# Moving the reciprocal root of the head norm to GpSimd, in a streaming encoder layer with matrix memory

## The reference, cut to what matters

```python
(C1, n1, m1), hm = mlstm_sequence(carry, (q, k, v, it, lf), n_lead)   # h = num / max(|den|, exp(-m))
mu = jnp.mean(hm, axis=-1, keepdims=True)
hc = hm - mu
hm = hc * lax.rsqrt(jnp.mean(hc * hc, axis=-1, keepdims=True) + EPS)
hm = hm.transpose(0, 2, 1, 3).reshape(B, L, D_M) * g_headnorm * o_gate
branch_m = hm @ w_branch_m
```

## Time and profile before

| what | value |
|---|---|
| time, median of 3 runs | 1316.61 us (1314.5 to 1318.08) |
| the profiled execution | 1317.66 us, span of its instructions 1315.9 us |
| PE / PEld / DVE / ACT / POOL busy | 97% / 92% / 57% / 29% / 2% |
| mean granted TensorE clock | 0.985 |
| table loads on ScalarE | 19, of 1.28 us each |

### The profile page before, as it was taken

One profiled execution on the slowest core, in us unless ns is written; L12 is line 12 of the kernel. 1 busy time (PEld: TensorE's weight loads), 2 busy tenths in 40 slices (PEclk: granted clock), 3 DMA queues, 4 the chain that ended last, 5 costly groups with the idle time before them and its releaser, 6 DMA issues.

```text
span 1315.9 us, 20235 instructions
## 1 busy us (share of the span) xinstructions
PE 1278.8 (97%) x7900; PEld 1204.3 (92%) x7900; DVE 745.2 (57%) x1327; ACT 387.4 (29%) x532; POOL 25.7 (2%) x40
## 2 busy tenths in 40 slices
PE   5999999999999999989999999999999999999997
PEld 4999999999999999989999898889889889989986
DVE  5442369786968696878846555434324334324463
ACT  4432133213321431131114723233213213312331
POOL 3000000000000000010000000000000000000000
PEclk8999999999999999999999999999999999999999
DMA  6242162316221622322232226112322222222321
GB/s 198 79 134 77 44 174 73 89 50 166 68 86 58 163 76 73 92 69 81 66 91 69 65 97 224 32 33 66 97 78 81 80 76 69 80 80 65 96 81 48
DMA packets 160397, 115.84 MB, mean 88 GB/s; under 512 B 13872, under 2 KB 148232, under 8 KB 160308
## 3 DMA queue, kind: packets, MB, share of 16 engines
q1 hardware_dynamic: 139124, 94.58, 24.8%
q10 hardware_dynamic: 21184, 20.02, 4.8%
HBM read 100.37 MB, written 14.21 MB: 87 GB/s over the span
## 4 chain that ended last, share of the span: by engine, by line
PE 92%; ACT 3%; DVE 2%; issue 2%; DMA 0%; POOL 0%; ACTq 0%; DVEq 0%; POOLq 0%; SPq 0%
PE out L357 42%; PE out L1547 28%; PE bank L1547 19%; PE bank L1542 3%; PE out L368 1%; ACT CV L617 1%; ACT GH L617 0%; DVE WL L312 0%; ACT WH L308 0%; ACT L617 0%; DVE WK L1043 0%; DVE XL L1011 0%; DVE CV L1014 0%; DVE WK L1014 0%; ACT WK L617 0%
## 5 line engine op out<-in xcount | busy, mean ns | idle before, releaser
L312 DVE TENSOR_TENSOR WL<-ST,WH 128x1024 fp32r<-128x1024 f32 x137 | 167.9, 1226 | 170.7 <-ACT WH L415 95.6
L357 PE MATMUL out<-XH,WH 128*128 128x328 f32 (+1 forms) x1024 | 242.7, 318 | 2.3 <-issue 2.3
L357 PE MATMUL out<-XH,WL 128*128 128x328 f32 (+1 forms) x1024 | 240.7, 316 | 0.0
L357 PE MATMUL out<-XL,WH 128*128 128x328 f32 (+1 forms) x1024 | 239.8, 315 | 0.0
L1014 DVE SCALAR_TENSOR_TENSOR CV<-WK,cwu,CV 128x512 f32 (+1 forms) x480 | 227.3, 547 | 0.4
L357 PEld LDWEIGHTS out<-XH,WH 128*128 128x128 f32 x1024 | 174.0, 190 | 3.4 <-issue 2.5
L357 PEld LDWEIGHTS out<-XH,WL 128*128 128x128 f32 x1024 | 174.0, 189 | 2.0 <-issue 1.3
L357 PEld LDWEIGHTS out<-XL,WH 128*128 128x128 f32 x1024 | 174.2, 189 | 0.9
L1011 DVE TENSOR_TENSOR WK<-WK 128x640 f32<-128x640 f32 (+7 forms) x78 | 64.7, 835 | 118.7 <-ACT WK L977 103.9
L1547 PE MATMUL bank<-WK 128*128 128x16 f32 (+8 forms) x752 | 126.8, 311 | 0.0
L1547 PE MATMUL out<-XH,WH 128*128 128x320 f32 (+2 forms) x512 | 120.1, 311 | 2.0 <-DVE WL L312 2.0
(11 more groups left out here) (212 smaller groups left out, 1591.0 us busy)
## 6 DMA issues: line engine op xcount, KB each, us to landing
ST<-in_w_in SPq DMA_DIRECT2D x65, 512.0 KB, 4.3
ST<-in_w_ff SPq DMA_DIRECT2D x64, 512.0 KB, 3.9
WK<-in_state_mlstm_C ACTq DMA_DIRECT2D x32, 256.0 KB, 3.0
o_C_sample<-WK ACTq DMA_DIRECT2D x32, 256.0 KB, 2.2
WK<-in_x_prompt SPq DMA_DIRECT2D x8, 512.0 KB, 5.8
ST<-in_w_branch_m SPq DMA_DIRECT2D x8, 512.0 KB, 4.3
ST<-in_w_branch_c SPq DMA_DIRECT2D x8, 512.0 KB, 4.1
ST<-in_w_out SPq DMA_DIRECT2D x8, 512.0 KB, 3.7
```

Of the source, the lines that this page charges most:

```text
L312: dve.tensor_tensor(WL[:, par % 2, :, :], ST[:, par % NSTAGE, :, :], WH[:, par % 2, :, :].bitcast(F32), ALU.subtract).then_inc(sem("w_lo"), 1)
L357: last = pe.matmul(out[s][:, h, 0:H], w[:, s, kk, :], x[:, kk, h * H:(h + 1) * H], start=(m < 2), stop=(m >= len(ms) - 2))
```

## The change

The four square roots on ScalarE and the four reciprocals on VectorE go; GpSimd raises the variance to the power -0.5 instead and writes the result where the root was. Its loop over the four heads is put between the roots of the first norm and the additions. VectorE's chain in the loop is shorter by one link.

```diff
-V_HEAD = 26
+V_HEAD = 25
...
+            for i in range(HEADS):
+                g.wait_ge(sem("hvar"), i + 1)
+                g.tensor_tensor(sm[:, 30:36], sm[:, 24:30], mhalf[:, :], ALU.pow).then_inc(sem("hrt"), 1)
 
             g.wait_ge(sem("conv"), 2 * TAPS * (HEADS - 1))
             g.wait_ge(sem("of0"), N_GM0 // 2 + 1)
...
-            def epilogue_root(i):
-                act.wait_ge(sem("hvar"), i + 1)
-                copy(sm[:, 30:36], sm[:, 24:30], "hrt", ACT.Sqrt)
...
-                else:
-                    epilogue_root(i - 1)
...
-                        if i == g == r == 0:
-                            epilogue_root(HEADS - 1)
...
                 dve.wait_ge(sem("hrt"), i + 1)
-                V.link(dve.reciprocal(sm[:, 18:24], sm[:, 30:36]))
-                V.link(tt(sm[:, 36:42], sm[:, 36:42], sm[:, 18:24], ALU.mult))
+                V.link(tt(sm[:, 36:42], sm[:, 36:42], sm[:, 30:36], ALU.mult))
```

## The result

| | before | changed |
|---|---|---|
| time, median | 1316.37 us (8 runs) | 1320.16 us (8 runs) |
| ratio | | 1.0032, 95% interval 1.0021 to 1.0042 |
| profiled execution; span | 1317.66; 1315.9 us | 1320.42; 1318.3 us |

The changed kernel is 3.8 us slower by the medians. That is within the 0.3% (3.95 us) that the prediction counted as no change, but the interval leaves out no change at all. The ratio is taken over all runs; the quotient of the two medians is 1.0029. The forecast was 3.3 us slower.

A forecast was written before the change was run, and what follows sets the result against it. TensorE was taken to bound the kernel (92% of the chain). Scalings 1.8 us later plus 1.5 us of lost clock made +3.3 us on the 1316.61 us median, giving 1319.9 us; range 1314.7 to 1321.5.

The forecast's parts named there:

- The loop costs nothing: Three heads ending in the loop: chain 0.95 us later per head, covered by 5.7 us before TensorE's transposes; cost nothing.
- Up to the variance: Last head: without additions beside it, VectorE's stretch takes 2.74 us instead of 5.51; the power ends at 561.97.
- The first addition wins against VectorE: Last head, after the power: GpSimd's first addition blocks VectorE's multiplication for 1.44 us, so it passes at 563.41.
- More additions between the scalings: Last head: further additions at 1.15 us each delay the scalings' end to 569.85, 1.8 us later than before.
- the two bounds: Last head's scalings end at 569.28 with three more additions (two operations a turn), 570.43 with four (one a turn).
- The wait: TensorE's wait for the last head's scalings grows from 1.5 us to 3.2 us.
- The clock: Behind TensorE's longer wait in the last head the granted clock falls, costing 1.5 us more.
- The sum: Whole kernel: 1.8 us from later scalings plus 1.5 us from the granted clock, 3.3 us slower, 1319.9 us.
- rival C: Last head: four more additions between the scalings and a clock loss of 1.7 us; +4.1 us, 1320.7 us; chance 0.12.
- Rival A: Last head: scalings stay together and hold off the additions; TensorE gains 1.7 to 1.1 us, 1315.1 us; chance 0.25.
- Rival B: Last head: additions come between the scalings but TensorE's clock holds; +1.8 us, 1318.4 us; chance 0.13.
- D: ScalarE's table loads are the price; removing five of 1.28 us gains 6.4 us, 1310.2 us; chance 0.02.

The follow-up runs named there:

- the run that removes them: Changed kernel with 24 useless matmuls keeping TensorE at work ahead of its wait for the last head's scalings; 1319.49 us, ratio 1.0025 to before.
- one move in TensorE's order: Last head's transposes moved from the middle to the end of gate tile 1: 1311.80 us on the kernel before, 1313.70 us on the changed kernel.
- three additions: Changed kernel with three of the five additions left on GpSimd, VectorE doing the other two after the gates; 1316.55 us, ratio 1.0003 to before.

## Why the prediction was right

- **The loop costs nothing.** Right. At the end of head 1 the power took 1.33 us (forecast 1.34), the scalings ended at 306.01 + 2.03 = 308.04 in the timeline of DVE, and the transposes came at 312.83. The kernel with the power in the loop alone has the time of before.
- **Up to the variance.** Right: 2.75 us instead of 5.51, and the power ended at 561.94, forecast 561.97.
- **The first addition wins against VectorE.** Right: the scalings began at 563.73. The forecast let the multiplication pass at 563.41 and the scalings begin 0.40 later, at 563.81.
- **More additions between the scalings.** Right in kind; the middle of the two bounds, 569.85, was a little low. The scalings ended at 570.08, one at each turn while additions ran, so all four additions came between them, as in the bound of 570.43. An addition cost 1.14 us, and the forecast took 1.15. The lower bound, 569.28, rested on two small operations getting through at each turn, and the timeline of DVE before doesn't bear that out. Between the three slowed operations it has:

```profile
560.53 0.17 DVE L1011 TENSOR_TENSOR sm<-sm,colH 128x6 f32<-128x6 f32 x1
560.61 0.49 DVE L1153 BATCH_NORM_AGGREGATE mv<-bst 16x2 f32<-16x6 f32 x6
561.14 0.19 DVE L1155 RECIPROCAL sm<-sm 128x6 f32<-128x6 f32 x1
...
561.94 0.17 DVE L1011 TENSOR_TENSOR sm<-sm 128x6 f32<-128x6 f32 x1
```

That is eight instructions in one turn and one in the other, and the slowed operations lost 1.1, 0.4 and 1.0 us, not the same each time. So it is partly luck that the middle came within 0.23 us. The Trainium skill (SBUF — State Buffer, "SBUF: two separate sides") says that a GpSimd instruction that has got the ports shared with VectorE keeps them to its end, and that a VectorE instruction that needs them is blocked until then. The trace agrees in that there was one slow scaling for each addition. A scaling lost 1.14 us while an addition took 1.44 (four in 5.74), so a block over the whole addition is not shown.

- **The wait.** TensorE waited 3.74 us, forecast 3.2. Most of the difference is the scalings, 0.23 us later than forecast, and that TensorE was free at 570.14 - 3.74 = 566.40, not at 566.62.
- **The clock.** The 1.5 us were 1.62 by the run that removes them. What the forecast left out is that a clock that falls here may not fall behind the next stall: in the profile of the changed kernel it stayed up there, in that of before it fell. That gave part of the loss back in that execution. Of the nine profiles whose next stall is 2.4 us long, the clock fell behind it in four. How often it does so in a kernel's other executions can't be read, since there is one profile of each.
- **The sum.** The step that was mis-sized is the wait: 1.8 us more than before were forecast, and 2.24 were measured. Beside that, the forecast put two things at nothing: nearly 0.4 us outside the span, and what the next stall gives back. Wait, clock and the time outside make 2.24 + 1.64 + 0.38 = 4.3 us, and the medians differ by 3.8. The missing 0.5 would fit the next stall, but no run shows that. So the misses partly cancel, and that the forecast of 3.3 lies so near is in part luck. In its mechanism, rival C (four more additions and a clock loss of 1.7; +4.1) is closer than the forecast. Rival A (the scalings hold the additions off) fell with the 6.35 us of the six scalings. Rival B fell with the clock of 0.56, and D with the loop's run: three table loads less there changed nothing.

## What to carry to other kernels

When work is moved to an idle engine, look first at what is queued behind it there: here one small operation of 1.3 us pushed 8 us of additions from a covered stretch into the chain that TensorE waited for. The additions and VectorE's scalings took turns, one instruction each. Beside an addition a short operation lost about as much as a long one: a copy took 1.30 us instead of 0.19, a scaling 1.54 instead of 0.40, a weight remainder 2.44 instead of 1.23. So several short ones lose more than one long one, though not every operation is slowed (the reciprocal above was not). And before making a late result earlier, see whether its consumer's order can be moved: one move in TensorE's order was worth more than either place of the root.

## What the runs showed beside this

The time outside the span of the instructions goes with the number of GpSimd's instructions in the page's first part, though not in proportion. With 40, 41 and 42 it is 1.72 to 1.75 us on average over a kernel's runs (before; the power in the last head only; three additions). With 43 (loop only) it is 1.90, and with 44 it is 2.11 to 2.13 (the changed kernel, and its runs with all powers and additions on GpSimd). The kernel before with four powers that nothing uses, put behind the additions, has 44 as well:

```profile
564.61 5.88 POOL L606 TENSOR_TENSOR spare<-ones,mhalf 128x6 f32<-128x6 f32 x4
```

> The kernel before, with four powers of 128x6 on GpSimd whose result nothing uses, behind its additions. In the runs so far the time outside the span of the instructions is 1.73 us for the kernel before, 1.90 with three powers on GpSimd and 2.11 with four. If the number of GpSimd's instructions sets it: 2.1 outside, and a time 0.4 over the kernel before. If something else of the change sets it (fewer instructions or table loads on ScalarE): 1.73, and no change.

It has 2.01 outside, where 2.1 was expected and the kernel before has 1.75 in the runs beside it; its time is the same within the interval, which is too wide to show 0.4 us. So of the changed kernel's 3.8 us nearly 0.4 lie where no row of the trace shows them. That the number of instructions goes with it is shown, and it isn't the powers alone: the kernel with three additions has four powers and stays at 1.74. Why, and whether it is the number or the length of the program, is open.
